# Router to first expert: squares by feature, gates after the selection, the second gather inside the first up-projection, expert blocks loaded as their places come free

## What is computed

```python
xl = xl + mod_l[2] * mixer_output(fl, gla_l, rw_l, ssd_l, p)      # residual after the projection
hl = modulate(rmsnorm(xl, norm2_g[i]), mod_l[3], mod_l[4])
xl = xl + mod_l[5] * moe(hl, p)
...
logits = (t @ p['router_w'] + p['router_b']).astype(jnp.float32)
top_v, top_i = lax.top_k(logits, TOP_K)                           # 4 of 32
probs = jax.nn.softmax(top_v, axis=-1)
gates = jnp.einsum('nk,nke->ne', probs, jax.nn.one_hot(top_i, N_EXPERTS, dtype=probs.dtype))
for e in range(N_EXPERTS):
    gu = t @ p['moe_w_gu'][e] + p['moe_b_gu'][e]                  # 1024 -> 2048
    glu, lin = jnp.split(gu, 2, axis=-1)
    glu, lin = jnp.minimum(glu, SWIGLU_LIMIT), jnp.clip(lin, -SWIGLU_LIMIT, SWIGLU_LIMIT)
    act = glu * jax.nn.sigmoid(SWIGLU_ALPHA * glu) * (lin + 1.0)
    y = y + gates[:, e:e + 1] * (act @ p['moe_w_down'][e] + p['moe_b_down'][e])
```

## Time and profile before

| | us |
|---|---|
| median of 3 runs | 1330.65 (1329.86 to 1331.6) |
| the profiled execution | 1328.54 |
| its span in the trace | 1326.6 |
| TensorE busy | 1245.0 (94%) |
| VectorE busy | 400.6 (30%) |
| ScalarE busy | 263.3 (20%) |
| expert weights and the rest read from HBM | 451.79 MB |

### The profile page before, as it was taken

How to read it: one execution, slowest core, us unless ns; L and a number is a source line. 1 busy time by engine, 2 the same in 40 slices (tenths; PEclk the granted TensorE clock), 3 DMA queues, 4 the chain that set the end, 5 groups by cost and what they waited for, 6 DMA issues and landing times.

```text
span 1326.6 us, 21403 instructions
## 1 busy us (share of the span) xinstructions
PE 1245.0 (94%) x9094; PEld 588.9 (44%) x9094; DVE 400.6 (30%) x896; ACT 263.3 (20%) x595; POOL 54.2 (4%) x88
## 2 busy tenths in 40 slices
PE   5999999989999999999999999999989999999987
PEld 3456666678885333333333333333333333333333
DVE  1555756755443111122111121211122111122112
ACT  2333208553324110011010011100111010011001
POOL 0031200311200000000000000000000000000000
PEclk9999999999999999999999999999999999999999
DMA  9673420142369999999999999999999999999995
GB/s 385 259 293 147 163 100 0 67 128 69 105 249 373 423 428 426 428 426 427 430 427 427 429 428 427 430 428 427 429 427 427 428 427 427 427 428 428 426 427 237
DMA packets 38378, 453.97 MB, mean 342 GB/s; under 512 B 4288, under 2 KB 4544, under 8 KB 10016
## 3 DMA queue, kind: packets, MB, share of 16 engines
q1 hardware_dynamic: 38304, 452.86, 82.0%
HBM read 451.79 MB, written 1.05 MB: 341 GB/s over the span
## 4 chain that ended last, share of the span: by engine, by line
PE 82%; DMA 8%; DVE 6%; issue 2%; ACT 1%; SPq 0%; DVEq 0%
PE PS L1965 79%; DMA arena<-in_moe_w_gu 5%; DMA arena<-in_moe_b_down 2%; PE PS L2852 1%; DVE arena L1858 1%; DMA arena<-in_ada_first 1%; DVE arena L1861 1%; DVE arena L1864 1%; PE PS L2843 1%; DVE arena L1335 1%; DVE arena L1857 1%; PE PS L2447 0%; DVE arena L1958 0%; PE PS L1977 0%; ACT arena L984 0%
## 5 line engine op out<-in xcount | busy, mean ns | idle before, releaser
L1965 PE MATMUL PS<-arena 128*64 128x512 f32 (+11 forms) x8790 | 1209.2, 415 | 41.1 <-DMA arena<-in_ada_first 15.0
L1965 PEld LDWEIGHTS PS<-arena 64*64 64x64 f32 (+6 forms) x8790 | 559.2, 148 | 642.3 <-issue 576.4
L1857 DVE TENSOR_SCALAR arena<-PS 128x256 f32<-128x256 f32 x64 | 38.7, 604 | 510.5 <-PE PS L1965 510.5
L1167 ACT ACTIVATE arena<-arena 128x256 f32<-128x256 f32 x64 | 26.7, 417 | 482.0 <-DVE arena L1857 482.0
L1886 DVE TENSOR_TENSOR arena<-PS,arena 128x512 f32<-128x512 f32 x32 | 22.2, 692 | 212.8 <-PE PS L1965 212.8
L1177 ACT COPY arena<-PS 128x256 f32<-128x256 f32 x32 | 11.9, 373 | 279.3 <-PE PS L2843 279.3
L2852 PE MATMUL PS<-arena 128*128 128x128 f32 x128 | 26.3, 287 | 32.6 <-DVE arena L1864 32.6
L1158 ACT ACTIVATE arena<-PS,arena 128x128 f32<-128x128 f32 x128 | 48.2, 457 | 35.6 <-PE PS L1965 35.6
L1335 DVE SCALAR_TENSOR_TENSOR arena<-PS,arena 128x255 f32<-128x255 f32 (+5 forms) x68 | 32.6, 481 | 28.5 <-ACT arena L971 19.5
L2852 PEld LDWEIGHTS PS<-arena 128*128 128x128 f32 x128 | 14.2, 141 | 59.9 <-DVE arena L1864 43.0
L1623 DVE COPY arena<-PS 128x384 f32<-128x384 f32 (+2 forms) x48 | 23.5, 491 | 52.7 <-PE PS L1965 52.3
(11 more groups left out here) (264 smaller groups left out, 388.6 us busy)
## 6 DMA issues: line engine op xcount, KB each, us to landing
arena<-in_moe_w_gu SPq DMA_DIRECT2D x125, 2048.0 KB, 24.9
arena<-in_moe_w_down SPq DMA_DIRECT2D x63, 2048.0 KB, 26.3
arena<-in_ada_rest SPq DMA_DIRECT2D x16, 1024.0 KB, 4.7
arena<-in_w_in SPq DMA_DIRECT2D x5, 2048.0 KB, 8.5
arena<-in_ada_first SPq DMA_DIRECT2D x4, 2048.0 KB, 19.4
arena<-in_moe_w_gu SPq DMA_DIRECT2D x24, 256.0 KB, 2.9
arena<-in_tokens SPq DMA_DIRECT2D x1, 2048.0 KB, 8.3
arena<-in_w_out SPq DMA_DIRECT2D x2, 1024.0 KB, 5.8
```

Source lines behind the costliest of these rows:

```text
L1167: act.activation(sgm[:, 256 * half:256 * half + 256], glu[:, 256 * half:256 * half + 256], ACT.Sigmoid, scale=ALPHA).then_inc(sig_ready, 1)
L1857: dve.tensor_scalar(by_rest(glu), of_half(0), LIMIT, None, ALU.min).then_inc(glu_ready, 1)
L1965: ins = pe.matmul(out, lhsT, rhs, start=start, stop=stop, skip_group_check=skip)
```

## The change

Five edits between the projection and the first expert. (1) The squares for the norm are taken from `xT` by ACT in feature-major form, and summed by TensorE with a matrix of ones into the second bank of `rt` (`squares_by_block`); the sums travel through `rs`, where ACT takes the root from PSUM and DVE the reciprocal. Both copies of `xk0`, `xk1` follow, then the exponential, whose table is no longer loaded ahead. (2) DVE makes positions and `select_pair(0)` before the gates; TensorE has `m5` behind `pos`; `gt` moves from pair 0 to pair 1. (3) `gather(1, 3)` stands in the first `up` ahead of `k` = 2, `gates_by_expert` ahead of `k` = 4, and `select_back` and the weighted bias behind it; the six filler matmuls are gone; ACT's `m5` copies and sigmoid table stand between its two gather copies. (4) SP loads block 3 when the last `mt` is drained, and expert 20's blocks when the last `ol` is. (5) Block 8 is loaded in two halves, the first when `k` = 0 of expert 0 is done.

```diff
@@ round_table
-    t += [("w0", 3, 1), ("w1", 0, 1), ("rt", 1, 1), ("xk0", 2, 1), ("xk1", 3, 1), ("m5", 1, 1), ("rs", 0, 1),
-          ("pos", 0, 1), ("gt", 0, 1), ...
+    t += [("w0", 3, 1), ("w1", 0, 1), ("rt", 1, 2), ("xk0", 2, 1), ("xk1", 3, 1), ("m5", 1, 1), ("rs", 0, 2),
+          ("pos", 0, 1), ("gt", 1, 1), ...
@@ SyncE
+            for d in range(2):
+                Q.emptied(sp, f"mt3{d}")
+            load_slot(3, 0, 3)
+            for d in range(2):
+                Q.emptied(sp, f"ol3{d}")
+            for x in range(2):
+                load_slot(RING + x, AHEAD * GROUP, 4 + x)
             Q.arrived(sp, "ro")
-            for r, e, s in ((3, 0, 3), (7, 1, 1), (RING, AHEAD * GROUP, 4), (RING + 1, AHEAD * GROUP, 5)):
-                load_slot(r, e, s)
+            load_slot(7, 1, 1)
...
-            for q in range(RING, PER * GROUP):
+            sp.wait_ge(half_freed, 1)
+            for x in range(2):
+                if x:
+                    sp.wait_ge(ring_free[0], 1)
+                at = slice(2048 * x, 2048 * x + 2048)
+                sp.dma_start(ring[0][:, at], gu_k[1:2, 2, :, :]...[:, at]).then_inc(ring_full[0] if x else block_parts, 16)
+            for q in range(RING + 1, PER * GROUP):
@@ ScalarE
-            for half in range(2):
-                for t in range(2):
...
-                    act.activation(h2k[:, t, at], pair(f"xk{t}")[:, at], ACT.Square, scale=D ** -0.5,
-                                   accum_out=by_half[:, 2 * half + t:2 * half + t + 1]).then_inc(sums_ready, 1)
-            act.wait_ge(sums_ready, 5)
-            act.activation(r2, r2, ACT.Sqrt).then_inc(root_ready, 1)
-            act.activation(small[:, 51:52], Cb(C_ONE)[:, 0:1], ACT.Exp)
+            R.emptied(act, "w0")
+            act.activation(squared[:, 0:4], xT[:, 0:4, :], ACT.Square).then_inc(sums_ready, 1)
+            act.wait_ge(router_in, 2)
+            act.activation(squared[:, 4:6], xT[:, 4:6, :], ACT.Square).then_inc(sums_ready, 1)
+            R.emptied(act, "w1")
+            act.activation(squared[:, 6:8], xT[:, 6:8, :], ACT.Square).then_inc(sums_ready, 1)
+            R.arrived(act, "rt")
+            R.drained("rt", act.copy(partial_squares, bank_of("rt")[:, 0:L]))
+            R.arrived(act, "rs")
+            R.drained("rs", act.activation(r2, bank_of("rs")[:, 0:2], ACT.Sqrt, scale=1.0 / D, bias=small[:, 57:58]))
...
             copy_gathered(0, 1, 0, 0)
+            block_gate()
             copy_gathered(1, 2, 0, 3)
@@ VectorE
-            dve.wait_ge(sums_ready, 4)
-            dve.scalar_tensor_tensor(out=r2, ...).then_inc(sums_ready, 1)
-            dve.wait_ge(root_ready, 2)
+            R.partly(dve, "rs", 1)
             run(dve.reciprocal(r2, r2))
...
+            select_pair(0)
             dve.wait_ge(rt_exp, 1)
             run(dve.tensor_tensor(gates, rt1, rt2, ALU.mult))
...
-            select_pair(0)
@@ TensorE
+            def squares_by_block(i):
+
+                pe.wait_ge(sums_ready, 1 + 2 * i)
+                for k in range(4 * i, 4 * i + 4):
+                    j = k % 4
+                    ins = mm(bank_of("rt")[32 * j:32 * j + 32, 0:L], Cb(C_ONE)[:, 0:32], squared[:, k, :], start=k < 4, stop=k >= 4, skip=True)
...
-                    if by_halves and k == 4:
-                        pe.wait_ge(hg_ready, n + 2)
-                        between()
+                    if first and k == 2:
+                        pe.wait_ge(late_in, 48)
+                        R.emptied(pe, "m5")
+                        gather(1, 3)
+                    if first and k == 4:
+                        gates_by_expert()
+                    if first:
+                        pe.wait_ge(hg_part, min(max(k, 3), 6))
+                        if k % 4 == 3 or k == 0:
+                            pe.wait_ge(hg_ready, k // 4 + 1)
...
+                    if first and k == 0:
+                        ins.then_inc(half_freed, 1)
...
-            keep_warm(6, 1)
             R.emptied(pe, "pos")
-            gates_by_expert()
             pe.wait_ge(block_parts, 16 * 28)
             pe.wait_ge(sel_ready, 4)
             gather(0, 0)
-            R.emptied(pe, "m5")
-            gather(1, 3)
-            R.emptied(pe, "gt")
```

## The result

The changed kernel took **1335.5 us** (median of 10 executions, 1330.3 to 1336.7) beside 1330.6 for the kernel before on the same chip: ratio 1.003, 95% interval 1.0018 to 1.0042, slower. A second set of 6 executions gave 1.0044 (1.0026 to 1.0061), so the loss is 0.3 to 0.45%, 4 to 6 us.

What follows compares the result with a forecast made beforehand. The weight stream was taken as the bound, released by expert 0's first down-projection block. `up` starting 3.75 us earlier, less 2.5 us paid back, gave 1.25 us: 1330.65 - 1.25 = 1329.4 us, range 1326.5 to 1333.2.

Steps and rivals of the forecast that it cites:

- slower rival: Recurrence's end: early loads cause another TensorE stall and clock fall, costing 3.7 us, so 1333.1 us; chance 13%.
- the sum: Up to expert 0's first down block: 3.75 us gained less 2.5 paid back, stream and end 1.25 us earlier, 1329.4.
- 1.25 us from which the rival was to decide: Recurrence's end: the stall length from which the slower rival, chance 13%, was to decide the outcome.
- buy nothing that is kept: Weight stream ahead of expert 0's down-projection: half block and early loads fill the ring sooner, but it empties no sooner.
- main chain: From the router's norm to expert 0's first up-projection: logits 1.5 us earlier, `up` at 406.4, 3.75 us earlier.
- clock rival: Ahead of expert 0's `up`: TensorE idles 1.7 us, the clock falls, costing 1.7 us, so 1331.1 us; chance 20%.
- block 9: Load during expert 0's `up`, delayed by the moved gather: forecast to be issued near 415.1.
- the empty stretch: Weight stream between block 8's data and block 9's: forecast 2.0 us with nothing flowing.
- Block 12: First load waiting for expert 0's down-projection, taken to limit the stream: issue forecast at 432.4 instead of 433.68.
- second term of the sum: Inside expert 0: TensorE pays back net 2.5 us for the moved gather and gates, leaving 1.25 of 3.75 us.

Runs made afterwards that it cites:

- e8_before_filled: The kernel before with eleven filler matmuls in expert 30's idle times, six ahead of the first turn and five ahead of the second: 1332.02 us, ratio 1.0001.
- e2_late_loads: The changed kernel with block 3, block 7 and expert 20's two blocks all issued behind the recurrence's last matmuls, as before: 1331.92 us, ratio 1.0002.

## Why the prediction was wrong

**The verdict.** Forecast 1329.4 in 1326.5 to 1333.2; it was 1335.5, slower. What came true was the slower rival, which had 13% and stood at 1333.1; the measured loss was larger still.

**The step that failed**: the sum has no term for what the early loads do to the recurrence. They stand in it with what they gain and at nothing for what they cost, and measured they cost 3.9 us of D and 4 to 6 us of the time. The reason for the nothing is in the rival, "Against it: the slice from 398 to 431 ran at 373 GB/s with TensorE's few waits all named". That slice lies behind the router, where TensorE does long matmuls: 56 in 10.24 us (the row at 414.15 below). The early loads went in beside rounds of small ones, 77 in 1.68 us, where the 256 instructions of a fetch are used up in 2.8 us of work. The row that spoke for that place was the earlier trace rows, 2.02 us without a releaser at loads under way; it was quoted, and given too little weight. The rival's mechanism (a stall without a releaser, and the lower clock behind it) was right, and its price of 3.7 us near; it was given too little chance. That it is the program's fetch which waits was not foreseen. D with the fetches in the same places is 12.42 to 13.60 with block 3 early (mean of four profiles 12.9) and 7.75 to 9.84 with it late (mean of seven 9.0), 3.9 us; the medians show 4 to 6, and the lower clock behind `ro` may be the rest. The clock is no sign of block 3 alone: it fell in this stretch in all four early profiles, but also in two of the seven late ones (`e2_late_loads` and `e8_before_filled`). The stall grew by 3.15 - 0.34 = 2.8 us over that of the kernel before, above the 1.25 us from which the rival was to decide.

The statement that the half block and the early loads "buy nothing that is kept" was right: with block 3 late the time is that of the kernel before (0.9999).

**The main chain, step by step**, each time less the 7.35 us by which the router's end was late. The rows of after, answering to the earlier trace rows:

```profile
403.54 0.42 DVE L1794 COPY arena<-PS 128x256 f32<-128x256 f32 x1 [1.41 <-PE PS L1979]
...
405.88 0.41 DVE L1799 SCALAR_TENSOR_TENSOR arena<-PS,arena 128x32 f32<-128x32 f32 x2
...
408.76 0.23 DVE L1819 SCALAR_TENSOR_TENSOR arena<-PS,arena 128x64 f32<-128x64 f32 x1 [1.00 <-PE PS L1979]
...
409.25 0.98 DVE L1828 TENSOR_SCALAR arena<-arena 128x64 f32<-128x64 f32 x4
...
412.50 1.50 ACT L1173 ACTIVATE arena<-PS,arena 128x128 f32<-128x128 f32 x4 [1.75 <-PE PS L1979]
...
414.15 10.24 PE L1979 MATMUL PS<-arena 128*64 128x512 f32 x56 [1.75 <-ACT arena L1173]
```

- Logits: 405.88 - 7.35 = 398.53, foreseen 398.55.
- `pos` read: 401.41, foreseen 401.4. `sel` complete: 410.23 - 7.35 = 402.88, foreseen 402.87.
- `up` starts at 406.80, foreseen 406.4: 0.4 late. And before it began at 410.05, not at 410.15, which was the start of ACT's second copies: so 3.25 us earlier, not 3.75. TensorE waits 1.75 us there, foreseen 1.7.
- The clock rival fell: the granted clock was 1.00 in 411 to 416 and after, behind the 1.75 us.
- The half block 408.77 (foreseen 408.2), block 9 at 416.06 (415.1), with the empty stretch (221 and 305 GB/s over 416 to 424, above).
- Block 12 at 433.32, foreseen 432.4. The gain is 0.36 us and not 1.25: this **second term of the sum was mis-sized**, by 0.9 us. 0.4 is the start of `up`. 0.4 is the moved gather: from the second half block, 417.83, to block 9 are 5.58 us, where the same part of `up` took 417.17 - 413.74 = 3.43, so a gather between two `k` steps costs 2.15, not the 1.73 that it took among its like. The prediction had named that price as unknown. The rest, 0.1, is the start of `up` before.

With block 3 late the gain of the router's part should be about 0.4 us by this one profile, and the kernel is not to be told from the one before (0.9999). So without the early block 3 the answer would have been "no change", inside the range.

**What stays open**: why a single 16 KB packet starts some 3 us late. The trace has its time under way at about 1 us (3.0% of 16 engines over 2 us, 0.96 us), also in the stall, so the delay is ahead of its start. That it starts as block 3 ends fits a packet that waits behind block 3's on its DMA engine, but the traces don't say which engine carries it, and the only other size tried is the quarter. Also open is how much of D's growth is stall and how much the clock that it lowers: in one execution 3.15 us and 1.7 ((1 - 0.72) x 2 + (1 - 0.71) x 4, some of it behind `ro`), with the early loads alone 2.3 us (1.12 + 1.21) and a clock of 0.58 over 12 us.

## What to carry over

A transfer that is "hidden anyway" isn't free where an engine works through short instructions: its program comes by DMA too, and here the next piece of it started only when the load beside it was nearly through. Before loads are moved into such a stretch, look for idle times without a releaser there, and for the packets of the instruction queue; count the instructions between two stalls. And where the time of such a kernel moves by a few tenths of a per cent with no reason in the diff, shift the program by half a fetch before believing in the edit: here the shift alone was worth 0.3%, 4 us, more than the 1.25 us that the change was forecast to gain.

## What the runs showed of the chip

- TensorE's program arrives in 16 KB packets, each 0.9 to 1.6 us under way, one for about 256 instructions (126 matmuls with their weight loads between two stalls). From 618 to 985 us the trace of the kernel before has none, which no run explains. TensorE can stand at each such boundary among 64x64 matmuls: up to 1.12 us ahead of the router with block 3 late, 2.88 to 3.15 us in three of four profiles with block 3's 2 MiB ahead (1.21 in the fourth, at half clock), and also up to 2.6 us further ahead, where only pieces of 256 KB are loaded. The Trainium skill (Trainium Architecture — The Big Picture, section The software stack) has the instruction streams moved to each engine when the program is loaded; the trace has 61 fetches during the execution, and the measurement decides.
- Inserting 128 instructions moved the boundary by 63 matmuls, inserting 256 put it back, and the time went with it.
- After the 3.15 us the granted clock was 0.71 to 0.72 in the mean of 382 to 388; in the second profile of the same kernel, with the same 3.15 us (375.86 to 379.01), it was 0.84 over 376 to 378 and 0.50, that is 1.2 GHz, over 378 to 384. How long TensorE stood is not what decides that alone: with the gates first 2.30 us at 365.09 left it at 1.00, and with block 3 late and the shift 1.70 us at 365.86 was followed by 0.50 over 368 to 370.
- A float32 matmul record of 8 columns behind its weight load takes 215 ns with 128 columns of weights and 56 ns with 32.
